# Expert stage of a two-layer decoder: the accumulating scatter becomes gather, add on GpSimd and plain scatter, and the experts run in another order

## The reference

```python
for layer in range(DEPTH):            # DEPTH = 2
    h = h + mixer(rms_norm(h, norm_mix[layer]))
    h = h + hier_moe(rms_norm(h, norm_ffn[layer]), ...)

def hier_moe(h, ...):                 # 4 groups x 8 experts, EXPERT_FF = 256
    gi = argmax(lg)                   # one group for each token
    top_p, top_i = top_k(softmax(le of that group), 2)   # two experts in that group
    # token rows are sorted by expert, each expert's rows padded to blocks of 128
    hid = silu(xb @ w_gate[e]) * (xb @ w_up[e])
    out = hid @ w_down[e]
    y = sum of the two expert rows of each token, times their gates
```

## Time and profile before

| what | value |
|---|---|
| median of 3 runs | 3121.38 us (3119.2 to 3127.32) |
| the profiled execution's own time | 3119.75 us |
| its span in the profile | 3117.8 us |
| TensorE busy | 2673.4 us (86%) |
| VectorE busy | 1747.1 us (56%) |
| ScalarE busy | 1260.4 us (40%) |
| GpSimd busy | 724.0 us (23%) |

### The profile page before, as it was taken

The page is one execution under the profiler, slowest core; times in us unless marked ns, Lnnn a source line. Parts: engine busy times, 40 slices in busy tenths (PEclk is TensorE's granted clock), DMA queues, the critical chain, the costliest instruction groups (busy, mean ns, idle before and its releaser), DMA issues. The chain is left out here.

```text
span 3117.8 us, 48627 instructions
## 1 busy us (share of the span) xinstructions
PE 2673.4 (86%) x15109; PEld 2236.8 (72%) x15112; DVE 1747.1 (56%) x3154; ACT 1260.4 (40%) x2369; POOL 724.0 (23%) x923
## 2 busy tenths in 40 slices
PE   5999979997968947998898599799879947989997
PEld 4999958875847836777676488578658836767775
DVE  4222246665755665667765366588733354676664
ACT  3222132225841104556654222288611104675653
POOL 1000023321110002444343143211100002444433
PEclk9999989998988968999999799899979968999998
DMA  6111112215536516899997322222154415999995
GB/s 243 50 56 52 40 60 78 75 65 165 163 121 234 194 61 216 261 301 302 316 281 228 118 87 80 91 83 88 53 198 143 149 39 179 298 359 285 283 308 132
DMA packets 175389, 509.57 MB, mean 163 GB/s; under 512 B 53800, under 2 KB 81456, under 8 KB 150320
## 3 DMA queue, kind: packets, MB, share of 16 engines
q1 hardware_dynamic: 142480, 393.69, 34.7%
q0 software_dynamic: 32800, 114.51, 15.4%
HBM read 374.56 MB, written 133.56 MB: 163 GB/s over the span
## 5 line engine op out<-in xcount | busy, mean ns | idle before, releaser
L1700 DVE TENSOR_TENSOR moe_parts<-expert_w,moe_parts 128x1024 fp32r<-128x1024 f32 x384 | 452.3, 1221 | 238.4 <-ACT moe_parts L1649 234.9
L1582 PE MATMUL ps<-moe_parts,moe_xT 128*128 128x512 f32 x2232 | 551.6, 403 | 23.0 <-issue 16.0
L1582 PEld LDWEIGHTS ps<-moe_parts,moe_xT 128*128 128x128 f32 x2232 | 418.1, 191 | 125.3 <-issue 20.5
L1649 ACT ACTIVATE moe_parts<-expert_w 128x1024 fp32r<-128x1024 f32 x384 | 373.3, 1047 | 80.3 <-PEq L155 78.8
L1109 PE MATMUL ps<-out_w,out_catT 128*128 128x512 f32 x1344 | 322.4, 399 | 14.2 <-DVE out_w L1265 11.8
L560 PE MATMUL ps<-in_gate_w,in_gate_hnT 128*128 128x384 f32 (+1 forms) x1536 | 319.4, 367 | 7.4 <-DVE in_gate_w L679 7.4
L1582 PE MATMUL ps<-moe_parts,moe_hidT 128*128 128x512 f32 x1116 | 289.0, 408 | 26.9 <-DVE moe_hidT L1713 24.2
L560 PEld LDWEIGHTS ps<-in_gate_w,in_gate_hnT 128*128 128x128 f32 x1536 | 278.7, 190 | 37.4 <-issue 7.5
L1109 PEld LDWEIGHTS ps<-out_w,out_catT 128*128 128x128 f32 x1344 | 255.7, 192 | 69.4 <-DVE out_w L1265 12.6
L560 PE MATMUL ps<-in_qk_w,in_qk_hnT 128*128 128x512 f32 x1152 | 268.4, 394 | 9.2 <-DVE in_qk_w L679 9.2
L1582 PEld LDWEIGHTS ps<-moe_parts,moe_hidT 128*128 128x128 f32 x1116 | 205.7, 191 | 76.2 <-DVE moe_hidT L1713 32.8
(11 more groups left out here) (262 smaller groups left out, 4150.8 us busy)
## 6 DMA issues: line engine op xcount, KB each, us to landing
expert_w<-in_w_gate SPq DMA_DIRECT2D x64, 1024.0 KB
expert_w<-in_w_up SPq DMA_DIRECT2D x64, 1024.0 KB
expert_w<-in_w_down SPq DMA_DIRECT2D x64, 1024.0 KB
hn_d<-out_hn SPq DMA_DIRECT2D x32, 512.0 KB, 2.6
in_gate_xt<-in_x SPq DMA_DIRECT2D x16, 512.0 KB
in_qk_xt<-in_x SPq DMA_DIRECT2D x16, 512.0 KB
att_k<-k_d SPq DMA_DIRECT2D x64, 128.0 KB, 2.9
out_ht<-in_x SPq DMA_DIRECT2D x16, 512.0 KB, 4.6
```

The costliest lines, as they stand in the source:

```text
L1582: last = nc.tensor.matmul(out, left[:, a, k, :], right(b, k), start=(n == 0 and k == 0), stop=(n == 2 and k == K_ - 1))
L1649: nc.scalar.activation(parts[:, j, 0, at], K.expert_w[:, j, at], ACT.Copy).then_inc(w_high.sem, 1)
L1700: nc.vector.tensor_tensor(parts[:, j, 1, at], K.expert_w[:, j, at], parts[:, j, 0, at].bitcast(F32), ALU.subtract).then_inc(w_low.sem, 1)
```

## The change

- The spare rows go: `h_d` and `out` have 2048 rows, and `setup` no longer writes zeros.
- A row without a token keeps an index beyond the last row. Gather, fetch and scatter have a bounds check that leaves such rows out. `K.who` goes, and `K.where` serves all three. `xg` and `acc` are cleared once.
- The scatter no longer adds. GpSimd fetches the block's residual rows of `h_d` into `acc`, adds `y` to give `z`, and scatters `z` plainly.
- `y_scaled` waits for the add of the block before (`summed`) instead of for a scatter to land, and reads its gates straight from `K.gates`.
- Expert order: expert 0 of each of the four groups, then expert 1 of each, and so on. `route` reorders the logits with four copies instead of one.
- The order on GpSimd in step m: gather m+2, wait for the fetch of m-1 and for scatter m-2, copy two columns, wait for `y_out` of m-1, add, scatter m-1, fetch m.

```diff
@@ route
-            leg = le[:, :, :].rearrange("p n (g e) -> p (n g) e", g=GROUPS)
-            go = gone[:, :, :].rearrange("p n g -> p (n g)").unsqueeze(2).broadcast_to([P, NT * GROUPS, EPG])
-            do(V.tensor_copy(le[:, :, :], lg[:, :, GROUPS:NL]))
+            turned_ = le[:, :, :].rearrange("p n (e g) -> p n e g", g=GROUPS)
+            for g in range(GROUPS):
+                own_.mark(V.tensor_copy(turned_[:, :, :, g], lg[:, :, GROUPS + g * EPG:GROUPS + (g + 1) * EPG]))
+            own_.meet()
+            leg = le[:, :, :].rearrange("p n (e g) -> p n e g", g=GROUPS)
+            go = gone[:, :, :].unsqueeze(2).broadcast_to([P, NT, EPG, GROUPS])
...
-            own_.mark(V.tensor_copy(K.who[:, :], found[:, 1, :]))
@@ experts, SyncE
-                load_expert(K, sp, layer, i * 2 + j, j, lambda n: alone(
-                    sp, w_low, i * (2 * PIECES) + ((j - 2) * PIECES + (n + 1) * PIECES // 3), K.tick_sp))
+                load_expert(K, sp, layer, j * EPG + i, j % 2, lambda n: alone(
+                    sp, w_low, i * (GROUPS * PIECES) + ((j - 2) * PIECES + (n + 1) * PIECES // 3), K.tick_sp))
@@ experts, GpSimd
+            def gather(m):
+                g.indirect_dma_start(xg[:, :], None, K.hn_d[layer], bass.IndirectOffsetOnAxis(ap=who[:, :], axis=0),
+                                     bounds_check=T - 1, oob_is_err=False).then_inc(gathered_s, 16)
+            def fetch(m):
+                g.indirect_dma_start(acc[:, :], None, K.h_d[layer], bass.IndirectOffsetOnAxis(ap=at[:, :], axis=0),
+                                     bounds_check=T - 1, oob_is_err=False).then_inc(acc_in, 16)
+            def add(m):
+                alone(g, y_out, m + 1, K.tick)
+                g.tensor_tensor(z[:, :], acc[:, :], y[:, :], ALU.add).then_inc(summed.sem, 1)
+                alone(g, summed, m + 1, K.tick)
             def scatter(m):
...
-                nc.gpsimd.indirect_dma_start(K.h_d[layer], bass.IndirectOffsetOnAxis(ap=where[:, :], axis=0), y[:, :], None,
-                                             compute_op=ALU.add).then_inc(scattered_s, 16)
+                g.indirect_dma_start(K.h_d[layer], bass.IndirectOffsetOnAxis(ap=where[:, :], axis=0), z[:, :], None,
+                                     bounds_check=T - 1, oob_is_err=False).then_inc(scattered_s, 16)
...
+            def step(m):
+                alone(g, x_turned, m + 2, K.tick)
+                g.tensor_copy(who[:, :], column(m + 2)).then_inc(who_set.sem, 1)
+                alone(g, who_set, m + 3, K.tick)
+                gather(m + 2)
+                g.wait_ge(acc_in, m * 16)
+                g.sem_inc(K.tick, 1)
+                g.wait_ge(scattered_s, m * 16)
+                g.sem_inc(K.tick, 1)
+                g.tensor_copy(where[:, :], column(m - 1)).then_inc(at_set, 1)
+                g.tensor_copy(at[:, :], column(m)).then_inc(at_set, 1)
+                add(m - 1)
+                g.wait_ge(at_set, m * 2 + 1)
+                g.sem_inc(K.tick, 1)
+                scatter(m - 1)
+                fetch(m)
@@ experts, ScalarE
             def y_scaled(m):
                 until(a, down, m + 1)
-                until(a, gated, m + 1)
-
-                a.wait_ge(scattered_s, m * 16 + 16)
-                nc.scalar.activation(y[:, :], yp, ACT.Copy, scale=gate[:, 0:1]).then_inc(y_out.sem, 1)
+                until(a, summed, m)
+                nc.scalar.activation(y[:, :], yp, ACT.Copy, scale=K.gates[:, bass.ds(m, 1)]).then_inc(y_out.sem, 1)
```

More of the change, by code:

```diff
@@ L186, in build @@
             self.o1_d = self.dram("o1_d", [T, D])
-            self.h_d = [self.dram("h_d", [T + P, D]), self.out]
+            self.h_d = [self.dram("h_d", [T, D]), self.out]
             self.hn_d = [self.dram(f"hn{i}_d", [T, D]) for i in range(2)]
@@ L232, in setup @@
         quarter = sb("quarter", [P, 1])
-        zeros = sb("zeros", [P, D])
-        pos_in, own, tab, sin_done, stored, made = (sem(n) for n in
-            ("pos_in", "own", "tab", "sin_done", "stored", "made"))
+        pos_in, own, tab, sin_done, stored = (sem(n) for n in ("pos_in", "own", "tab", "sin_done", "stored"))
         pool_own = sem("pool_own")
@@ L243, in _ @@
             sp.dma_start(place, src).then_inc(there, 16)
-            sp.wait_ge(made, 1)
-            for h in K.h_d:
-                sp.dma_start(h[T:T + P, :], zeros[:, :]).then_inc(stored, 16)
             sp.wait_ge(sin_done, 2)
             sp.dma_start(K.rope_d.rearrange("(n p) c -> p n c", p=P), table[:, :, :]).then_inc(stored, 16)
-            sp.wait_ge(stored, 48)
+            sp.wait_ge(stored, 16)
         @block.gpsimd
@@ L1042, in step @@
                 alone(sp, added, n + 1, K.tick_sp)
-                sp.dma_start(rows(K.h_d[layer][0:T], n), h2[:, j, :]).then_inc(st, 16)
+                sp.dma_start(rows(K.h_d[layer], n), h2[:, j, :]).then_inc(st, 16)
                 if s.plus(2).within(NT):
@@ L1066, in _ @@
             for e in range(2):
-                load_expert(K, sp, layer, e, e)
+                load_expert(K, sp, layer, e * EPG, e)
             step(s0.plus(1))
@@ L1478, in experts @@
         y = sb("y", [P, D])
-        who, where = sb("who", [P, 1], I32), sb("where", [P, 1], I32)
-        gate = sb("gate", [P, 1])
+        acc, z = sb("acc", [P, D]), sb("z", [P, D])
+        who, at, where = (sb(n, [P, 1], I32) for n in ("who", "at", "where"))
         parts = sb("parts", [P, 2, 2, EW], F32R)
         gathered_s, scattered_s = sem("gathered"), sem("scattered")
-        who_set, where_set = Count(sem("who_set")), Count(sem("where_set"))
+        acc_in, at_set = sem("acc_in"), sem("at_set")
+        cleared, who_set = sem("cleared"), Count(sem("who_set"))
         x_turned, x_high, x_low = Count(sem("x_turned")), Count(sem("x_high")), Count(sem("x_low"))
@@ L1521, in load @@
             def load(i, j):
-                load_expert(K, sp, layer, i * 2 + j, j, lambda n: alone(
-                    sp, w_low, i * (2 * PIECES) + ((j - 2) * PIECES + (n + 1) * PIECES // 3), K.tick_sp))
-            with sp.Fori(1, NE // 2) as i:
-                for j in range(2):
+                load_expert(K, sp, layer, j * EPG + i, j % 2, lambda n: alone(
+                    sp, w_low, i * (GROUPS * PIECES) + ((j - 2) * PIECES + (n + 1) * PIECES // 3), K.tick_sp))
+            for j in range(2, GROUPS):
+                load(0, j)
+            with sp.Fori(1, EPG) as i:
+                for j in range(GROUPS):
                     load(i, j)
@@ L1534, in _, with column @@
         def _(g):
+            def column(m):
+                return K.where[:, m:m + 1] if isinstance(m, int) else K.where[:, bass.ds(m, 1)]
             def gather(m):
[L1536 to L1539, removed]
@@ L1553, in _ @@
+            g.sem_inc(summed.sem, summed.credit)
+            g.memset(xg[:, :], 0.0).then_inc(cleared, 1)
+            g.memset(acc[:, :], 0.0).then_inc(cleared, 1)
+            g.tensor_copy(who[:, :], column(0)).then_inc(who_set.sem, 1)
+            g.tensor_copy(at[:, :], column(0)).then_inc(at_set, 1)
+            g.wait_ge(cleared, 2)
+            until(g, who_set, 1)
             gather(0)
             g.dma_start(where[:, :], K.where[:, 0:1]).then_inc(scattered_s, 16)
-            g.wait_ge(gathered_s, 16)
@@ L1558, in _ @@
[L1558 to L1561, removed]
+            g.wait_ge(at_set, 1)
+            fetch(0)
+            for m in (1, 2):
+                until(g, x_turned, m)
+                g.tensor_copy(who[:, :], column(m)).then_inc(who_set.sem, 1)
+                until(g, who_set, m + 1)
+                gather(m)
+            def step(m):
[14 more added lines that the diff above has]
+                fetch(m)
@@ L1562, in _ @@
             total = end_of(g, NE)
             with g.Fori(1, total) as m:
[L1564 to L1569, removed]
+                step(m)
+            g.wait_ge(acc_in, total * 16)
+            g.sem_inc(K.tick, 1)
+            g.wait_ge(scattered_s, total * 16)
+            g.sem_inc(K.tick, 1)
+            g.tensor_copy(where[:, :], column(total - 1)).then_inc(at_set, 1)
@@ L1570, in _ @@
+            add(total - 1)
+            g.wait_ge(at_set, total * 2)
+            g.sem_inc(K.tick, 1)
             scatter(total - 1)
```

20 lines of the change are left out of this document (5 added, 15 removed).

## The result

The changed kernel takes 3324.3 us, median of 4 runs (3314.74 to 3327.12), against 3120.9 for the kernel before, run with it: a ratio of 1.0636, 95% interval 1.0617 to 1.0655. It is 203 us slower, where 58 us were forecast.

What follows compares the result with a forecast made beforehand. The prediction took transfers to bound much of the expert stages' 10.86 us blocks beyond TensorE's 9.56. GpSimd's new 11.4 us loop gave 91 x (11.4 - 10.86) = +49, plus 9: 3178 us, range 3130 to 3280.

Steps and rivals of the forecast that it cites:

- The loop on GpSimd: Expert stages: each block waits serially for fetch landing, copies, add, scatter and next fetch; 11.4 us a block.
- The sum: GpSimd's serial steps per block: 0.24 + 0.5 + 2.6 + 0.83 + 1.3 + 5.9 = 11.37 us; ends 9.3 and 17.5.
- Rival 3: Expert stages: GpSimd's add holds up VectorE's subtractions, VectorE becomes the bound; 192 us over forecast, or 96 (3274 us); chance 0.10.
- Against: no row shows GpSimd and VectorE holding each other up on wide operands: Argument against VectorE becoming the bound in the expert stages, a case given chance 0.10.
- The signs of being wrong that it named: Adds waiting for `y_out`, subtractions well over 1.22 us, or a bounds-checked gather or scatter holding GpSimd over 1.6 us.
- Afterwards a scatter has a whole block more before anyone needs it: Expert stages: claimed relief from the scatter's loop of y, issue and landing, 8.4 to 11.7 us before the change.
- What was removed: Expert stages: the scatter's add and y's wait for it, rows without a token, one copy a block (1.74 us).
- the upper bound: Most the removals could gain: period falls to TensorE's 9.56 us, 91 x 1.30 = 118 us.
- Rival 2: Expert stages: the fetch lands as slowly as now, 7.6 us instead of 5.9; period 13.1, 3333 us; chance 0.15.
- Edges: Outside the block periods: layer starts 4 us, layer ends 5, route's copies 1, setup at most -1; together +9.

## Why the prediction was right in direction and wrong in size

**The loop on GpSimd: right.** The longest wait is that for `acc`, as forecast, the DMA share fell from 0.89 to 0.67, and TensorE waits for gathers. Two buffers alone, which take this loop away, give 135 us back.

**Its size: wrong, and this is the step that failed.** The sum took the terms around the add (copies 0.5, scatter to fetch 1.3, landing 5.9) as if VectorE's subtractions did not hold GpSimd up there; its ground was that no row showed it. With VectorE's second SBUF operand gone, the same loop measures 11.49 us, where the sum had 11.37, and the kernel 3191 us, where 3178 were forecast. With it, 13.02. The difference of 1.5 us a block lies in the copies and the wait for y (0.93 against 0.33), in scatter to fetch (1.95 against 1.35) and in landing (6.65 against 6.35). The add itself, the one term to which contention had been charged, is hardly longer: 2.41 against 2.38, because it mostly begins first (only 4 of the 93 took over 2.6 us) and it is the subtraction that waits. On the kernel the contention is 133 us. Part of the nearness of 11.49 to 11.37 is luck: landing and add's end to scatter came out 0.2 longer each than forecast, copies and add 0.2 shorter each.

**Rival 3: the right mechanism, at too low a chance, with the wrong consequence.** It let contention matter only by making VectorE the bound. VectorE did not become the bound in the kernel after, where the waits for `acc` lead. TensorE waited most for VectorE where GpSimd has no such loop: with the extra add in the kernel before, and with two buffers. In the kernel after the delays went into GpSimd's own short instructions, which are links of the loop. The Trainium skill (SBUF — State Buffer, Who interferes with whom) says that a VectorE instruction with two SBUF inputs contends with a GpSimd instruction that reads SBUF, and not with one that only writes. The traces agree: subtractions of 1838 ns beside the add, 1221 beside the memset.

**"Against: no row shows GpSimd and VectorE holding each other up on wide operands": missed.** Rows with a wide subtraction and a narrow copy were there. In the earlier trace rows the index copy takes 0.94 us at 2881.52, in the earlier trace rows the same copy takes 0.18 and the gate's copy 1.74. VectorE's timeline of the kernel before, at those moments:

```profile
2876.97 2.38 DVE L1700 TENSOR_TENSOR moe_parts<-expert_w,moe_parts 128x1024 fp32r<-128x1024 f32 x2 [2.93 <-ACT moe_parts L1649]
...
2880.07 2.35 DVE L1700 TENSOR_TENSOR moe_parts<-expert_w,moe_parts 128x1024 fp32r<-128x1024 f32 x2
```

The gate's copy ends at 2877.65 + 1.74 = 2879.39, the first pair at 2879.35; the index copy ends at 2882.46, the second pair at 2882.42. A copy of one column that takes ten times its time and ends with another engine's instruction is what contention looks like. The forecast had read the 1.74 as the copy's own cost behind a scatter. It was so all through the kernel before: in its expert stages index copies took 0.18 us in each of the 44 cases with no subtraction beside them, and 0.77 in the mean of the 52 with one.

**The signs of being wrong that it named.** Two of the three came: subtractions of 1453 ns, and scatters that held GpSimd 2.04 us in the median of layer 1. The second is not the bounds check, since with one SBUF operand in the subtraction the same scatter took 1.04.

**"Afterwards a scatter has a whole block more before anyone needs it": false.** It is issued late in step m and awaited in step m+1. In the kernel after, that is hidden behind the fetch, which goes out later; with the fetch first or absent it is the wait that binds. The reordering tried on single buffers stayed at 12.40 us, and even without a fetch the period was 11.84.

**What was removed: worth less than the upper bound.** Leaving out the rows without a token gave 0.3%, the room for y nothing more. The forecast's 5.9 us for the fetch counted on a third fewer rows; what loads the landing is the weights (4.94 to the next copy without most of them, 6.65 with).

**The two losses overlap.** Against the kernel after, opening the loop gives 135 us, ending the contention 133, both together 225, not 268. That would follow if a delay counts in full in a loop and in part behind a buffer; it was not tested further.

**Rival 2** had the period (13.1) almost exactly, and for the wrong reason: its landing of 7.6 us, 7.84 to the next copy, is measured at 6.65. A time that fits a rival doesn't speak for its mechanism; only the terms do.

**Edges**: 9 us forecast. The medians leave 203 - 194 = 9, the profiled executions 207 - 194 = 13; the single edges were not checked.

## What to carry to other kernels

Before work goes to GpSimd, list the VectorE instructions with two SBUF operands that will run beside it, and look in the trace for short GpSimd instructions that end with them. Copies, adds and DMA issues of GpSimd all waited for such instructions here. Fetch, change and scatter through single buffers make a loop that holds every landing, so write down for each wait in which step its transfer was issued. The add was cheapest where the data had to be read anyway, in the instruction that empties PSUM.

## What the hardware showed

- GpSimd and VectorE held each other up for whole instructions. In the timelines above a one-column copy took 0.18 or 1.25 us, an indirect DMA's issue 1.03 or 2.05, two subtractions 2.36 or 3.90, depending on what the other had begun.
- Without any GpSimd add of full width the subtractions were back at 1223 ns, but they still held GpSimd: its scatters lasted up to 2.09 us beside the add of 64 columns, and 2.05 with no add at all.
- A plain scatter of up to 128 rows of 4 KB holds GpSimd 1.04 us undisturbed, the accumulating one 1.60.
- In the kernel after, with no weights loading, the next copy came 4.5 us after a fetch of 2 rows with a token was issued (at 1767.47), and 5.0 after one of 128 (at 3301.79). The longest landing, 18.3 us in layer 0, lay beside the 5 MB load for the next stage.
- TensorE's granted clock over the stages, a mean between its levels as a share of the full 2.4 GHz, fell from 0.98 and 1.00 to 0.91 and 0.92, with TensorE idle for longer between blocks; with the loop opened and the contention ended it was 0.98 and 1.00 again. What the clock alone cost was not measured.
